# Rope columns of the second block from the raw residual in four f32 column groups, and the next chunk rounded in quarters

## The reference

```python
h = modulate(rmsnorm_2(x, g_attn_norm[l]), sh_a, sc_a)     # h * (1 + scale) + shift
proj = jnp.dot(h, w_in[l])
q_lat, kv_lat, k_rope, ca_qkv = jnp.split(proj, split_pts, axis=-1)   # 256, 128, 32, 1536 columns
...
k = rmsnorm_2(jnp.concatenate([k_nope, broadcast(k_rope)], axis=-1), g_mla_k[l])
k = jnp.concatenate([k[..., :64], rope(k[..., 64:], positions)], axis=-1)
```

## Time and profile before

| | us |
|---|---|
| median of 3 runs | 1175.96 (1175.93 to 1176.64) |
| the profiled execution | 1176.15 |
| its span | 1174.4 |
| PE busy | 1162.8 |
| DVE busy | 562.0 |
| ACT busy | 516.0 |
| POOL busy | 465.1 |

### The profile page before, as it was taken

How to read it: one execution, slowest core, us unless ns; L and a number is a source line. 1 busy time by engine, 2 the same in 40 slices (tenths; PEclk the granted TensorE clock), 3 DMA queues, 4 the chain that set the end, 5 groups by cost and what they waited for, 6 DMA issues and landing times.

```text
span 1174.4 us, 16056 instructions
## 1 busy us (share of the span) xinstructions
PE 1162.8 (99%) x5922; PEld 951.0 (81%) x5922; DVE 562.0 (48%) x1120; ACT 516.0 (44%) x817; POOL 465.1 (40%) x189
## 2 busy tenths in 40 slices
PE   9999999999999999999999999999999999999998
PEld 7787778988888888888988666789888888888887
DVE  4364245977777774212574576726434334430000
ACT  5534653634444442322546577835443443431110
POOL 6541314344434433444443314044434443434442
PEclk9999999999999999999999999999999999999999
DMA  8222122544554542223332110122233223212222
GB/s 309 109 86 94 36 103 78 215 185 174 213 199 168 205 157 87 96 98 110 131 132 92 55 37 1 37 72 78 102 107 107 73 106 107 81 64 99 99 98 96
DMA packets 27715, 132.06 MB, mean 112 GB/s; under 512 B 3473, under 2 KB 4881, under 8 KB 18833
## 3 DMA queue, kind: packets, MB, share of 16 engines
q1 hardware_dynamic: 25776, 128.90, 30.8%
q10 hardware_dynamic: 1888, 2.49, 0.7%
HBM read 129.28 MB, written 2.10 MB: 112 GB/s over the span
## 4 chain that ended last, share of the span: by engine, by line
PE 96%; ACT 2%; DVE 1%; issue 1%; POOL 0%; DMA 0%; DVEq 0%; ACTq 0%
PE psum L1576 86%; PE psum L1657 2%; PE psum L1645 2%; PE psum L2100 1%; PE psum L1806 1%; PE psum L1909 1%; ACT prob L731 1%; DVE prob L1274 0%; ACT probT L714 0%; PE psum L2010 0%; POOL wl L497 0%; DMA gains_and_h<-x_first 0%; PE psum L1874 0%; PE psum L2047 0%; DVE prob L1291 0%
## 5 line engine op out<-in xcount | busy, mean ns | idle before, releaser
L481 POOL TENSOR_TENSOR wl<-raw,wh 128x2048 fp32r<-128x2048 f32 (+1 forms) x88 | 364.5, 4142 | 497.1 <-ACT wh L647 285.0
L1576 PE MATMUL psum<-xh,wh 128*128 128x512 f32 (+1 forms) x1008 | 382.9, 380 | 1.1 <-POOL wl L497 1.1
L1576 PE MATMUL psum<-xh,wl 128*128 128x512 f32 (+1 forms) x1008 | 378.6, 376 | 0.0
L1576 PE MATMUL psum<-xl,wh 128*128 128x512 f32 (+1 forms) x1008 | 378.6, 376 | 0.0
L1225 DVE SCALAR_TENSOR_TENSOR scratch<-psum,cols,scratch 128x511 f32<-128x511 f32 (+1 forms) x176 | 131.6, 748 | 195.4 <-ACT scratch L792 186.4
L1576 PEld LDWEIGHTS psum<-xh,wh 128*128 128x128 f32 x1008 | 189.5, 188 | 40.5 <-issue 3.1
L1576 PEld LDWEIGHTS psum<-xh,wl 128*128 128x128 f32 x1008 | 189.6, 188 | 34.2
L1576 PEld LDWEIGHTS psum<-xl,wh 128*128 128x128 f32 x1008 | 189.7, 188 | 34.1 <-issue 0.2
L647 ACT ACTIVATE wh<-raw 128x2048 fp32r<-128x2048 f32 (+1 forms) x50 | 88.4, 1768 | 243.9 <-PE psum L1576 243.9
L1576 PE MATMUL psum<-acth,wh 128*128 128x512 f32 (+1 forms) x374 | 141.0, 377 | 0.0
L1576 PE MATMUL psum<-actl,wh 128*128 128x512 f32 (+1 forms) x374 | 140.8, 377 | 0.0
(11 more groups left out here) (272 smaller groups left out, 1379.2 us busy)
## 6 DMA issues: line engine op xcount, KB each, us to landing
raw<-stream SPq DMA_DIRECT2D x69, 1024.0 KB, 4.7
ada_raw<-ada SPq DMA_DIRECT2D x48, 512.0 KB, 5.2
raw<-down SPq DMA_DIRECT2D x32, 704.0 KB, 4.0
outT<-gains_and_h SPq DMA_DIRECT2D x8, 256.0 KB, 5.0
gains_and_h<-xT SPq DMA_DIRECT2D x7, 256.0 KB, 5.9
raw<-stream SPq DMA_DIRECT2D x7, 256.0 KB, 6.4
rel<-rel_tiles ACTq DMA_DIRECT2D x1, 1344.0 KB, 8.7
wsT<-w_spatial_T SPq DMA_DIRECT2D x1, 512.0 KB, 6.0
```

Source lines behind the costliest of these rows:

```text
L481: pool.tensor_tensor(wl[slot][:, 0:w], raw[slot][:, 0:w], wh[slot][:, 0:w].bitcast(F32), ALU.subtract).then_inc(lo_done, 1)
L1576: ins = pe.matmul(out, lhs[a], rhs[b], start=first and n == 0, stop=last and n == 2)
```

## The change

The rope columns leave the weight stream. Their 32 columns come in a small array of their own (`w_rope`, with a 128x128 matrix that adds the four groups and places the exchanged columns), loaded by ScalarE's queue into `scratch[0]` ahead of the down projection. GpSimd multiplies them with `modA`. PE multiplies the raw columns with the shifts (8 matmuls of one column, into bank 3) at the start of the last half tile, and the scaled columns with the raw residual `h` (8 f32 matmuls of 512, bank 4) before k = 6 of the second half of the first pair. ScalarE copies the parts to `scratch[2]`, VectorE multiplies them with the root of the norm, ScalarE adds the shifts, and one f32 matmul with the placing matrix gives the rope tile in bank 2, in the middle of the ql tile. The first chunk holds kv and the first ql tile, the second only the second ql tile (1024 columns). Chunk base + 2 is rounded in quarters ahead of the final norm's root and of the loads of the biases, and GpSimd subtracts it by quarters. VectorE makes the third latent low part behind the rope work, no longer ahead of it.

```diff
-STREAM2 = [("kvr", 1), ("ql", 1), ...
+STREAM2 = [("kvq", 1), ("ql", 1), ...
 def chunk_width(n):
-    if n == BASE2["mkv"]:
+    if n in (BASE2["ql"], BASE2["mkv"]):
         return CHUNK // 2
...
@@ GpSimd
             lows(N1, base - 1, DOWN_CHUNK)
+            pool.wait_ge(pos_landed, 32)
+            pool.wait_ge(mod_done, 7)
+            pool.tensor_tensor(rope_weights..., rope_raw..., modA[:, 0, :]..., ALU.mult).then_inc(mod_done, 1)
...
-            lows(base + 2, BASE2["mkv"])
+            low_edge(base + 2, 10)
+            lows(base + 3, BASE2["mkv"])
@@ ScalarE
             act.dma_start(pos_i, positions.partition_broadcast(P)).then_inc(pos_landed, 16)
+            act.dma_start(scratch[0][:, 0:ROPE_COLS + P], w_rope[:, :]).then_inc(pos_landed, 16)
...
             norm_rsqrt(norm_attn2, 0, eps2_c)
+            act.wait_ge(p2.mm, P2["shift"])
+            act.activation(rope_shift[:, :], SHIFTS, ACT.Copy).then_inc(rope.act, 1)
...
+            act.wait_ge(p2.mm, P2["rope_parts"])
+            act.activation(scratch[2][:, :], rope_parts[:, :], ACT.Copy).then_inc(rope.act, 1)
+            act.wait_ge(rope.dve, 2)
+            act.wait_ge(rope.act, 1)
+            act.activation(scratch[2][:, :], scratch[2][:, :], ACT.Identity, bias=rope_shift[:, :]).then_inc(rope.act, 1)
+            base = N1 + N_DOWN
+            for x in range(4):
+                split_quarter(base, x, p2.mm, P2["ql"][0], True)
+            act.wait_ge(norm_final.ss, 1)
+            rsqrt(ss_acc[:, :], SS_FINAL[:, :], D, eps_c, norm_final.rstd, 0)
             act.wait_ge(res_down1.h, KD + 1)
             load_rel(0, 0, 2)
             load_rel(1, 2, HEADS)
-            act.wait_ge(norm_final.ss, 1)
-            rsqrt(ss_acc[:, :], SS_FINAL[:, :], D, eps_c, norm_final.rstd, 0)
...
-            split_next(base, p2.mm, P2["rope"])
...
             head_square(sq2[0][:, :], bank[0][:, :], P2["kv"])
-            act.activation(sqk[0][0:96, :], bank[1][0:96, :], ACT.Square).then_inc(rope.sq, 1)
+            head_square(sq2[1][:, :], ql_tiles[0][:, :], P2["ql"][0])
             lat_square_high(0, sq2[0])
-            head_square(sq2[1][:, :], bank[2][:, :], P2["ql"][0])
+            lat_square_high(1, sq2[1])
+            act.wait_ge(p2.mm, P2["rope"])
+            act.activation(sqk[0][0:96, :], rope_tile[0:96, :], ACT.Square).then_inc(rope.act, 1)
+            act.wait_ge(rope.act, 4)
+            act.activation(rope_sq[0:96, :], sqk[0][0:96, :], ACT.Copy).then_inc(rope.act, 1)
...
@@ VectorE
+            dve.wait_ge(rope.act, 2)
+            for j in range(2):
+                dve.tensor_tensor(scratch[2][:, half(j)], scratch[2][:, half(j)], rstd(j), ALU.mult).then_inc(rope.dve, 1)
...
-            for b, sq in enumerate((sq2[0], sq2[1], scratch[3])):
-                lat_square_low(b, sq)
+            lat_square_low(0, sq2[0])
+            lat_square_low(1, sq2[1])
             (rope products, k_rope, low part of the rope squares, copy)
+            lat_square_low(2, scratch[3])
@@ TensorE
+            def quarter_products(out, columns, moving, ready, value):
+                pe.wait_ge(ready, value)
+                for x in range(KD // QUARTERS):
+                    for quarter in range(QUARTERS):
+                        k, c = QUARTERS * x + quarter, GATE_COLS * quarter
+                        ins = pe.matmul(out[c:c + GATE_COLS, :], columns[:, GATE_COLS * k:GATE_COLS * k + GATE_COLS], moving(k),
+                                        start=x == 0, stop=x == KD // QUARTERS - 1)
+                return ins
...
+                        if (j, e, kk) == (1, 0, 0):
+                            quarter_products(SHIFTS, rope_raw, lambda k: mod[:, 0, k:k + 1], mod_done, 8).then_inc(p2.mm, 1)
...
+            def rope_products():
+                pe.wait_ge(norm_attn2.lo, 2 * KD - 2)
+                quarter_products(rope_parts, rope_weights, lambda k: h[:, k, :], mod_done, 8).then_inc(p2.mm, 1)
-            normed_pair(bank[0:2], base % 2, p2.mm, norm_attn2, last_sums, 5, KD + 6)
+            normed_pair(bank[0:2], base % 2, p2.mm, norm_attn2, last_sums, 5, KD + 6, rope_products)
             pe.wait_ge(lo_done, base + 2)
-            for e in range(2):
-                features_tile(bank[2 + e], (base + 1) % 2, e).then_inc(p2.mm, 1)
+            pe.wait_ge(rope.dve, 2)
+            for k in range(KD):
+                if k == KD // 2:
+                    pe.wait_ge(rope.act, 3)
+                    pe.matmul(rope_tile[:, :], rope_turned, scratch[2][:, :], start=True, stop=True).then_inc(p2.mm, 1)
+                ins = split_product(ql_tiles[1][:, :], weights((base + 1) % 2, P * k, P * k + P), inputs(k), k == 0, k == KD - 1)
+            ins.then_inc(p2.mm, 1)
```

More of the change, by code:

```diff
@@ L49 @@
 STREAM1 = [("ua", 1), ("vg", 2), ("ub", 1), ("v", 2), ("qk", PAIRS), ("out", KD // 2), ("up", KF)]
-STREAM2 = [("kvr", 1), ("ql", 1), ("cqk", PAIRS), ("cv", 2), ("mq", 1), ("mkv", 1), ("out", KD // 2), ("up", KF)]
+STREAM2 = [("kvq", 1), ("ql", 1), ("cqk", PAIRS), ("cv", 2), ("mq", 1), ("mkv", 1), ("out", KD // 2), ("up", KF)]
 N1 = sum(n for _, n in STREAM1)
@@ L118, in build @@
         minus_rq = sb("minus_rq", [P, 2 * STEPS])
-        sb("to_row", [P, ROW_PAD])
+        rope_shift = sb("rope_shift", [P, 1])
+        sb("to_row", [P, ROW_PAD - 1])
         gains_and_h = sb("gains_and_h", [P, GAINS + KD * T])
@@ L288, in build @@
         rope = Stage()
-        rope.dve, rope.sq = sems("rope", "dve", "sq")
+        rope.dve, rope.act = sems("rope", "dve", "act")
         head = Stage()
@@ L302, in build @@
               "q": [17, 19, 21, 23], "k": [18, 20, 22, 24]}
-        P2 = {"kv": 1, "rope": 2, "ql": [3, 4], "q": [5, 7, 9, 11], "k": [6, 8, 10, 12], "v_first": 13, "v": [14, 15, 16, 17]}
+        P2 = {"shift": 1, "rope_parts": 2, "kv": 3, "ql": [4, 6], "rope": 5, "q": [7, 9, 11, 13], "k": [8, 10, 12, 14],
+              "v_first": 15, "v": [16, 17, 18, 19]}
         MLA = {name: n + 1 for n, name in enumerate(
@@ L375, in build @@
         CSIL_HALVES = [ss_final, bank[7]]
+        ROPE_COLS = KD * GATE_COLS
+        rope_raw, rope_turned = scratch[0][:, 0:ROPE_COLS], scratch[0][:, ROPE_COLS:ROPE_COLS + P]
+        rope_weights = scratch[1][:, 0:ROPE_COLS]
+        rope_parts = bank[4]
+        rope_tile = bank[2]
+        SHIFTS = bank[3][:, 0:1]
+        ql_tiles = [bank[1], bank[3]]
         gate_raw, gate_weights = [lf[b][:, 0:KD * GATE_COLS] for b in range(2)]
@@ L608, in rope_keys @@
                     pool.wait_ge(mla.k_rope, 2 * p + e + 1)
-            pool.wait_ge(rope.dve, 5)
+            pool.wait_ge(rope.dve, 7)
             pool.wait_ge(lo_done, n)
@@ L968, in _ @@
             head_square(sq2[0][:, :], bank[0][:, :], P2["kv"])
-            act.activation(sqk[0][0:96, :], bank[1][0:96, :], ACT.Square).then_inc(rope.sq, 1)
+            head_square(sq2[1][:, :], ql_tiles[0][:, :], P2["ql"][0])
             lat_square_high(0, sq2[0])
-            head_square(sq2[1][:, :], bank[2][:, :], P2["ql"][0])
+            lat_square_high(1, sq2[1])
[3 more added lines that the diff above has]
+            act.activation(rope_sq[0:96, :], sqk[0][0:96, :], ACT.Copy).then_inc(rope.act, 1)
             act.wait_ge(norm_attn2.lo, 2 * KD)
-            head_square(scratch[3][:, :], bank[3][:, :], P2["ql"][1])
-            lat_square_high(1, sq2[1])
+            head_square(scratch[3][:, :], ql_tiles[1][:, :], P2["ql"][1])
             lat_square_high(2, scratch[3])
             split_next(base + 1, p2.mm, P2["ql"][1])
-            act.wait_ge(rope.sq, 1)
-            act.activation(rope_sq[0:96, :], sqk[0][0:96, :], ACT.Copy).then_inc(rope.sq, 1)
             head_root(JOB_KV, P, bank[4])
@@ L1459, in lat_square_low @@
                 dve.tensor_tensor(lat_low[b][:, :], sq[:, :], lat_high[b][:, :].bitcast(F32), ALU.subtract).then_inc(head.lo, 1)
-            for b, sq in enumerate((sq2[0], sq2[1], scratch[3])):
-                lat_square_low(b, sq)
+            lat_square_low(0, sq2[0])
+            lat_square_low(1, sq2[1])
             dve.wait_ge(trig.row, 2)
[L1464 to L1469, removed]
+            dve.wait_ge(rope.act, 4)
+            dve.tensor_tensor(rope_tile[64:P, :], rope_tile[64:P, :], k_trig[64:P, :], ALU.mult).then_inc(rope.dve, 1)
+            dve.tensor_tensor(turn[64:P, :], rope_tile[0:64, :], k_trig[0:64, :], ALU.mult).then_inc(rope.dve, 1)
+            dve.wait_ge(rope.dve, 4)
+            dve.tensor_tensor(k_rope[64:P, :], rope_tile[64:P, :], turn[64:P, :], ALU.add).then_inc(rope.dve, 1)
+            dve.wait_ge(rope.act, 5)
             dve.tensor_tensor(rope_sq[96:P, :], sqk[0][64:96, :], rope_sq[64:96, :].bitcast(F32), ALU.subtract).then_inc(rope.dve, 1)
-            dve.wait_ge(rope.dve, 3)
+            dve.wait_ge(rope.dve, 5)
             dve.tensor_copy(k_rope[0:64, :], k_rope[64:P, :]).then_inc(rope.dve, 1)
+            lat_square_low(2, scratch[3])
             def head_rstd(job):
@@ L1592, in features_tile, with normed_pair @@
```

(14 more changed lines are left out.)

15 lines of the change are left out of this document (8 added, 7 removed).

## The result

| | before | after |
|---|---|---|
| median of 22 runs | 1176.14 us (1175.72 to 1176.72) | 1177.76 us (1176.64 to 1179.04) |
| profiled execution | 1176.15 | 1176.96 |
| its span | 1174.4 | 1175.2 |

A forecast was written before the change was run, and what follows sets the result against it. PE was taken as the bound, busy 1162.8 of 1174.4 us. Added 3.8 less removed 5.45 gave -1.65; with -0.14, +0.05 and +0.1 that made -1.6, so 1175.96 became 1174.4 us, range 1173.3 to 1177.0.

The forecast's parts named there:

- the 24 matmuls that go: One of four feature tiles on PE disappears: 24 matmuls at 0.227 us, 5.45 us less.
- the rope products: Eight f32 matmuls of 512 columns before k = 6 of the first pair's second half: 2.05 us more on PE.
- the turn: One f32 matmul, 128x512, for the turn and quarter sum: 0.86 us more on PE.
- the near-meeting at chunk cqk0: GpSimd finishes cqk0's quarters at 591.15, PE asks at 591.2; cover 0.1 us, wait taken as 0.1 us.
- the shifts: Eight one-column f32 matmuls, 16 instructions, on PE: 0.9 us, taken between 0.3 and 1.8.
- the product with rstd: VectorE multiplies the rope parts in two halves; PE's wait for it 0 to 0.2 us, taken as 0.05.
- the milder form of rival A: Only the last latent low part is caught behind GpSimd: PE waits 2.4 us, time 1176.8; both forms together 0.13.
- a series that is running keeps its way: On VectorE before the latent sums: GpSimd is held off while a VectorE series runs; counted against rival A, chance 0.13.
- rival A's full form: Rope square's and last latent low parts both caught behind GpSimd: PE waits 3.5 us, 1177.9; both forms together 0.13.
- the lower end, 0.3: Lower bound for the shifts on PE, from 32-column weight loads: 16 x 0.02 = 0.3 us.
- The estimate of 0.4 us: Alternative price for the shifts on PE: 16 instructions at about 60 cycles (25 ns) overhead, giving a balance of -2.15 us.

The follow-up runs named there:

- e1: The changed kernel with VectorE's third latent low part back directly behind the second, ahead of the rope operations: 1174.79 us, ratio 0.9988.
- e2: The changed kernel with the third latent low part between k_rope and the rope square's low part: 1174.67 us, ratio 0.9990.
- e6: The changed kernel with GpSimd subtracting chunk cqk1 in four pieces of 512 columns instead of one of 2048: 1174.57 us, ratio 0.9988.
- e3: The changed kernel with the four loads of the relative biases issued behind the rounding of chunk cqk1: 1175.60 us, ratio 0.9995.
- e8: e2 with sixteen one-column VectorE memsets added behind the norm tiles of the second block: 1174.54 us, ratio 0.9986.
- e4: The changed kernel once more, unchanged, to see the slower group of its times: one run, 1178.52 us.
- e5: The changed kernel with nine more 512-column matmuls between the first latent sum and the wait for the third low part: 1177.08 us.
- e7: The kernel before the change with two one-column VectorE memsets added behind the norm tiles of the second block: 1176.39 us, ratio 1.0004.

## Why the prediction was wrong

*What held.* The bound (PE), the 24 matmuls that go and their price (PE reaches cqk0 1.86 us earlier for 1.6), the rope products (2.05) and the turn (0.86) to the hundredth, the near-meeting at chunk cqk0 (0.06 us), and the claim that nothing else around the change costs. Where the lock, the pair of ports that VectorE and GpSimd share, holds up nobody for whom PE waits (e1, e2, e6), the kernel takes 1174.57 to 1174.79 us against the 1174.4 of the forecast. That this is so close is in part luck: the shifts cost 0.47 us less than priced, and against that stand 0.17 more for the product with rstd and the 0.37 of the gap at 805 us, which the forecast did not have.

*The step that failed* is the one on VectorE: "the copy to 597.0, and the last latent low part, 597.0 to 597.7. That is 2.2 us ahead of PE's wish." What happened is the milder form of rival A, for which with the full form the prediction had a chance of 0.13. Its mechanism, place and length were as written (2.4 us foreseen, 2.22 measured); the order in which the two engines come, and with it the chance, were wrong. Two things put it there.

The first is a price. The prediction gave the copy 0.3 us and named no row for it. The trace of before has it:

```profile
602.84 0.42 DVE L1472 COPY k_rope<-k_rope 64x512 f32<-64x512 f32 x1
```

With 0.42, and 0.03 to the next operation, the low part comes at 597.15 in the old clock, behind GpSimd's 597.1 and not ahead of it. With the 0.43 of the shifts that is 597.58 and 597.53; measured are 597.62 and 597.59. Even so a forecast with errors of some hundredths can't settle a race of 0.03 us.

The second is the sentence "a series that is running keeps its way", read from one pair of rows, which made the race look harmless. e2, e3 and e8 show that it does not hold here: GpSimd, come while VectorE's series ran, went ahead of the copy. In the earlier trace rows the four operations of L1353 overlap (2.49 us for four of 0.69); here each waits on a semaphore and stands 0.03 to 0.04 us behind the one before. That this is what makes the difference fits all the traces, but no run tried it.

The rule of the Trainium skill ("SBUF — State Buffer", SBUF: two separate sides), by which whoever starts first has the pair of ports for one instruction, agrees with the traces: a low part that came second took 5.10 us behind one piece of 2048 columns (the changed kernel) and 1.81 behind one of 512 (e6), and GpSimd came in between two operations in e2.

*The order on VectorE was the cause.* Before, the third low part stood ahead of the rope operations, and the one that was caught was L1470, for which nobody waited. The change put the critical one behind. With the old order alone, and the loads where the change has them, the wait is gone (e1); with the loads moved and the new order it is 0.6 us (e3).

*What was missing from every case* is the clock. I priced PE's stand-still by its length. In half of the executions it costs 1.6 us more, because PE runs at 1.2 GHz for 3.4 us behind it (e4), and none of it is left when the wait is filled (e5). Without it the time would have been about 1176.9 (the median of the lower group) or 1177.1 (e5): at the upper end of the range, 1177.0, and still slower than before where faster was forecast. That the median, 1177.76, lies near the 1177.9 of rival A's full form is chance: that form has two operations caught one after the other, and here only one was.

*Sizes.* The shifts cost 0.43 us and not 0.9: the 0.11 us that one matmul of L1839 takes with 128-column weights is no price for 32 columns, and the lower end, 0.3, was the nearer one. The estimate of 0.4 us from the Trainium skill ("TensorEngine Tiling (Array Packing)", Instruction Overhead) was right to 0.03. The wait for the product with rstd was 0.22 for 0.05: the product was done at 585.38, just as PE was due (585.39), and the rest is the hand-over and PE's slower start (585.53 for the first matmul, 585.84 for the second). The gap of 0.37 us at 805 us was in no sum. Together: -1.86 at cqk0, +2.22 at the sums, +0.37 at 805 is +0.7, of the +0.8 between the spans.

## What to carry to other kernels

Look in the old trace at which operation is caught behind GpSimd, and who waits for it: here the order that lets the one be caught for which nobody waits was worth 2.2 us, more than the 1.6 that the change was to save. Where two chains come to the same lock within a tenth of a microsecond, count it as lost, and put the one on the critical path first, or cut the other into pieces. Price an operation from its own row, and where a race hangs on it, name the row. Price a new stand-still of an otherwise busy TensorE with the clock that may fall behind it, not with its length alone.

## What the runs showed of the hardware

- A stand-still of PE of 1.92 us was followed by 3.4 us at a granted clock of 1.2 GHz, 1.6 us longer (rows of e4; by time and mean clock in 11 of 22 executions of the changed kernel). With the wait filled by nine matmuls (e5) and with one of 0.6 us (e3) no run of 11 had it, and a stand-still of 1.28 us elsewhere left the clock at 1.00.
- A VectorE operation of 128x512 or 32x512 with two SBUF inputs that started while GpSimd subtracted ended 0.55 or 0.56 us behind it (before, changed kernel, e1), which made it 5.10 us for 0.69 where it came 0.03 us late. Behind GpSimd's piece of 512 columns it took 1.81 (e6).
- A VectorE copy in f32 from SBUF to SBUF (64x512) is caught like an operation with two inputs: 4.72 us for 0.42 (e2, e3, e8).
- Sixteen matmul instructions of one column with 32-column weights, in four column groups, cost 0.43 us in all; the same sixteen with 512 columns 2.05.
- VectorE lost 0.37 us at one instruction with two instructions more in front of it, and not with sixteen more (e7 and e8, one trace each).
